# Ten gated branch tiles split inside the head pairs and loaded back as halves; the sum over positions as adds; a new order in the last pair

## The reference

```
h = rms_norm(x) ; z = h @ w_in                       # 2048 -> 6144: u, g_pool, q, k, v, g_attn
pool branch : mean over the last 2/4/8/16 positions - u, a 256x256 map per group, scale, * silu(g_pool)
attn branch : 16 heads x 64, keys at distances 0, d, 2d, .. <= window for (128,1), (512,4), (2048,16),
              penalty -slope*distance, the three patterns weighted by their softmax sums, * silu(g_attn)
x = x + [pool ; attn] @ w_out ; y = rms_norm(x)
```

## Time and profile before

| what | value |
|---|---|
| median of 3 runs | 886.05 us (885.88 to 886.07) |
| the profiled execution's own time | 882.29 us |
| its span, first to last instruction | 880.5 us |
| PE busy | 850.8 us (97%) |
| DVE, ACT, POOL busy | 557.0 us (63%), 396.0 us (45%), 35.0 us (4%) |
| mean granted TensorE clock | 0.988 of full |
| DMA traffic | 117.13 MB, mean 133 GB/s |

### The profile page before, as it was taken

How to read it: one execution, slowest core, us unless ns; L and a number is a source line. 1 busy time by engine, 2 the same in 40 slices (tenths; PEclk the granted TensorE clock), 3 DMA queues, 4 the chain that set the end, 5 groups by cost and what they waited for, 6 DMA issues and landing times. The chain is left out here.

```text
span 880.5 us, 17273 instructions
## 1 busy us (share of the span) xinstructions
PE 850.8 (97%) x6974; PEld 843.1 (96%) x6974; DVE 557.0 (63%) x1067; ACT 396.0 (45%) x917; POOL 35.0 (4%) x62
## 2 busy tenths in 40 slices
PE   7999999999999999999999999999798999999993
PEld 7999999999999999999999999999788999999993
DVE  5646885696678569757956774787788443333333
ACT  5745435524543453355245434533445453433332
POOL 3000000000000000000000000000000000000001
PEclk9999999999999999999999999999899999999997
DMA  9476257337524733663376247326454433433425
GB/s 305 124 144 164 82 144 175 94 93 177 153 73 107 197 107 96 159 151 95 90 177 158 79 126 176 106 77 167 118 167 145 125 111 112 125 113 109 141 65 194
DMA packets 205063, 117.13 MB, mean 133 GB/s; under 512 B 6232, under 2 KB 200288, under 8 KB 204960
## 3 DMA queue, kind: packets, MB, share of 16 engines
q1 hardware_dynamic: 202712, 111.20, 46.8%
q0 software_dynamic: 2272, 4.83, 1.6%
HBM read 103.93 MB, written 12.53 MB: 132 GB/s over the span
## 5 line engine op out<-in xcount | busy, mean ns | idle before, releaser
L578 PE MATMUL pj<-mov_hi,w_hi 128*128 128x260 f32 x1952 | 404.3, 288 | 0.0
L578 PE MATMUL pj<-mov_hi,w_lo 128*128 128x260 f32 x1952 | 393.7, 283 | 0.0
L578 PE MATMUL pj<-mov_lo,w_hi 128*128 128x260 f32 x1952 | 393.1, 283 | 0.0
L578 PEld LDWEIGHTS pj<-mov_hi,w_hi 128*128 128x128 f32 x1952 | 301.5, 189 | 0.9
L578 PEld LDWEIGHTS pj<-mov_lo,w_hi 128*128 128x128 f32 x1952 | 302.0, 189 | 0.0
L578 PEld LDWEIGHTS pj<-mov_hi,w_lo 128*128 128x128 f32 x1952 | 301.7, 189 | 0.0
L1180 DVE TENSOR_TENSOR w_lo<-w_raw,w_hi 128x768 fp32r<-128x768 f32 (+1 forms) x189 | 163.4, 865 | 180.8 <-ACT w_hi L797 179.9
L797 ACT ACTIVATE w_hi<-w_raw 128x768 fp32r<-128x768 f32 (+1 forms) x189 | 145.5, 770 | 200.5 <-PE pj L578 170.0
L853 ACT ACTIVATE pt_hi<-ps_t 128x128 fp32r<-128x128 f32 (+1 forms) x64 | 26.2, 435 | 69.7 <-PE ps_t L607 67.0
L1263 DVE TENSOR_TENSOR pt_lo<-ps_t,pt_hi 128x128 fp32r<-128x128 f32 (+1 forms) x64 | 29.6, 483 | 36.5 <-ACT pt_hi L853 36.5
L845 ACT ACTIVATE arena<-arena,stat 128x128 f32<-128x128 f32 (+1 forms) x64 | 34.2, 558 | 35.2 <-DVE stat L1257 35.1
(11 more groups left out here) (210 smaller groups left out, 801.7 us busy)
## 6 DMA issues: line engine op xcount, KB each, us to landing
w_raw<-in_w_in SPq DMA_DIRECT2D x96, 320.0 KB, 3.5
w_raw<-in_w_in SPq DMA_DIRECT2D x48, 384.0 KB, 3.5
arena<-in_cache_k_win SPq DMA_DIRECT2D x16, 384.0 KB
arena<-in_cache_v_win SPq DMA_DIRECT2D x16, 384.0 KB
w_raw<-in_w_out SPq DMA_DIRECT2D x16, 384.0 KB, 3.3
w_raw<-in_w_out SPq DMA_DIRECT2D x16, 320.0 KB, 3.0
arena<-in_cache_k_win SPq DMA_DIRECT2D x8, 512.0 KB
arena<-in_cache_v_win SPq DMA_DIRECT2D x8, 512.0 KB
```

The lines of the kernel that those rows point to most:

```text
L578: mm = pe.matmul(dst[h][:, 0:HT], w, m[:, k, HT * h:HT * h + HT], start=(k == 0 and i == 0), stop=(c == 2 and k == KT - 1 and i == 2))
```

## The change

1. Ten branch tiles (`STAGED`) are split inside the pairs. ACT copies the tile into `stg_hi` (`stage_hi`), DVE subtracts into `stg_lo` (`stage_lo`), and POOL stores both to DRAM (`send_split`). ACT waits with the next one until both stores of the one before have landed. In the order of pairs: tile 8 (stored in pair 1), 9, 10, 3, 11, 12, 4, 5, 13, 14. Tiles 4, 5 and 13 all come in pair 6, at places 3, 5 and 8; tile 14 comes in pair 7 at place 8.
2. SP loads these halves back straight into `mov_hi` and `mov_lo` (`load_split`): places 3, 4, 5 at step 143, 6, 7, 8 at 144, 9, 10 at 145, 13, 14 at 146. Each group waits until the chunk that last reads these places is done.
3. Three tiles (0, 1, 2) still come through `mix_scratch` and are split at steps 142 (two) and 143 (one).
4. `value_sum` becomes six adds in two parts, at places 22 and 23 (before: 22).
5. In all pairs the key loads are issued at places 5, 6 and 7, and the two small exponentials of the sample rows on ACT go from ahead of the weight split to behind it.
6. In pair 7 the plan is new.

```
-SPLIT_ORDER = (0, 1, 2, 3, 4, 5, 6, 7, 8, 9, 10, 13, 14, 11, 12, 15)
-RELOADED = (0, 1, 2, 3, 4, 5, 6, 7, 8, 9, 10, 13, 14)
-MIX_BUFS = 6
+SPLIT_ORDER = (0, 1, 2, 11, 12, 15)
+RELOADED = (0, 1, 2)
+STAGED = (8, 9, 10, 3, 11, 12, 4, 5, 13, 14)
...
-             vm=(20, 21, 21), vr=22, av=24, pick=25, mix=(19, 21), gate=20)
-FINAL = Plan(qk=(7, 11), s=(8, 12), kn=13, ur=14, kq=(9, 10, 11), ns=15, pt=17,
-             vm=(12, 13, 14), vr=15, av=18, pick=20, mix=(17, 18), gate=19)
+             vm=(20, 21, 21), vr=(22, 23), av=24, pick=25, mix=(19, 21), gate=20)
+FINAL = Plan(qk=(7, 11), s=(8, 12), kn=13, ur=14, kq=(8, 9, 10), ns=17, pt=19,
+             vm=(13, 14, 14), vr=(18, 20), av=20, pick=21, mix=(17, 18), gate=19)
...
+            def load_split(i):
+                k = OUT_K[i]
+                c = 0 if i < 6 else (1 if i < 11 else 2)
+                sp.wait_ge(stg_st, 32 * len(STAGED))
+                sp.wait_ge(w_used, IN_CHUNKS - 1 + c)
+                sp.dma_start(mov_hi[:, i, :].bitcast(F32), hi_dram[k]).then_inc(mov_in[i], 16)
+                sp.dma_start(mov_lo[:, i, :].bitcast(F32), lo_dram[k]).then_inc(mov_in[i], 16)
...
-                    if j in (6, 7, 8):
-                        load_keys(pr, j - 6)
+                    if j in (5, 6, 7):
+                        load_keys(pr, j - 5)
...
+                for i in {-1: (3, 4, 5), 0: (6, 7, 8), 1: (9, 10), 2: (13, 14)}.get(n, ()):
+                    load_split(i)
...
-                        pe.wait_ge(m_split, after_split(k))
+                        if k in mov_in:
+                            pe.wait_ge(mov_in[k], 32)
+                        else:
+                            pe.wait_ge(m_split, after_split(k))
...
+            def stage_hi(k, src):
+
+                e = STAGED.index(k)
+                if e > 0:
+                    act.wait_ge(stg_st, 32 * e)
+                act.activation(stg_hi[:, :], src, ACT.Copy).then_inc(stg_hi_done, 1)
...
+            def send_split(k):
+                pool.wait_ge(stg_split, STAGED.index(k) + 1)
+                pool.dma_start(hi_dram[k], stg_hi[:, :].bitcast(F32)).then_inc(stg_st, 16)
+                pool.dma_start(lo_dram[k], stg_lo[:, :].bitcast(F32)).then_inc(stg_st, 16)
...
+            def add_positions(pr, i, to, n, other):
+
+                out = av if to is None else vv[:, P * to:P * (to + n)]
+                to = to or 0
+                if i > 0:
+                    dve.wait_ge(av_add, 5 * pr + i)
+                o = dve.tensor_tensor(out, vv[:, P * to:P * (to + n)], vv[:, P * other:P * (other + n)],
+                                      ALU.add)
+                o.then_inc(av_add if i < 5 else av_done, 1)
+
+            def value_sum(pr, half):
+
+                if half == 0:
+                    dve.wait_ge(pv_s, 3 * pr + 3)
+                    add_positions(pr, 0, 0, 10, 10)
+                    return
+                add_positions(pr, 1, 0, 5, 5)
+                add_positions(pr, 2, 0, 2, 2)
+                add_positions(pr, 3, 0, 1, 1)
+                add_positions(pr, 4, 0, 1, 4)
                 if pr > 0:
                     dve.wait_ge(av_sum, pr)
-                dve.tensor_reduce(av, vv.rearrange("p (s x) -> p x s", x=P), AX_X,
-                                  ALU.add).then_inc(av_done, 1)
+                add_positions(pr, 5, None, 1, POS - 1)
...
+            def stage_lo(k, src):
+                dve.wait_ge(stg_hi_done, STAGED.index(k) + 1)
+                dve.tensor_tensor(stg_lo[:, :], src, stg_hi[:, :].bitcast(F32),
+                                  ALU.subtract).then_inc(stg_split, 1)
```

131 lines of the change are left out of this document (58 added, 73 removed).

## The result

The changed kernel takes **871.86 us** (median of four runs, 871.21 to 872.39), against 885.96 us for the kernel before on the same chip (four runs, 884.14 to 886.07). The ratio is 0.9845, with a 95% interval of 0.9828 to 0.9862: 14.1 us less, where 9.0 were forecast, and 0.6 us outside the range. A rerun on another chip gave 871.94 against 883.89 us, ratio 0.9866 (0.9851 to 0.9882), which is 12.0 us. The changed kernel repeats; the kernel before does not. Most of this part of the document is about that difference.

The account below looks back on a forecast made before the run. PE bounds the kernel, busy 97% of the span, and loses time only to waits and slow clock in pair 7. 2.7 + 2.0 + 1.4 + 2.9 = 9.0 us off the median of 886.05 gave 877.05 us, range 872.5 to 882.0.

Parts of the forecast that it names:

- Staged tiles: Copies and subtracts of ten tiles move into pairs 1 to 7; counted 0, bounds 0 and 1.2 us lost.
- Loads into the operand in time: Twenty transfers of 260 KB replace ten and arrive before chunks 144 and on want them; counted 0.
- Adds: Six adds replace the sum over positions on DVE: about 3.5 us instead of 4.9, counted 0 for PE.
- Gap 2: PE's wait of 1.99 us in pair 7 up to 659.84, behind a late DVE reciprocal; goes, 2.0 us.
- the cap of 13.4 us: All that pair 7 loses in waits and slow clock; nothing the change touches can be worth more.
- gap 3: PE's wait of 2.89 us in pair 7 up to 668.50, for `pooled_lo` from DVE; goes, 2.9 us.
- gap 1: PE's wait of 5.31 us in pair 7 up to 635.91; 2.7 us shorter, between 2.0 and 3.3.
- The clock: Slow stretches behind pair 7's first two waits lose 1.8 and 1.4 us; counted 0 and 1.4 us saved.
- All of pair 7's losses go: Rival: early key load, no slow stretch, DVE stays ahead; 13.4 us less, or 872.6; 13%.
- The key load no faster: Rival: PE stalls one unit earlier in pair 7, its first wait isn't shortened; about 4 us, or 882; 14%.
- the loads into the operand late: Rival: chunk 147 waits for places 6 to 10 and it ends slower; 896 at 120 GB/s; 5%.
- the mere shuffle: Rival: DVE's list is only shuffled, and what leaves three spots delays three others as much; 886; 6%.

Follow-up runs that it names:

- The keys alone: The kernel before with key loads (all pairs) and the last pair's key products a place earlier, nothing else: 879.84 us, ratio 0.9957.
- The fillers: Useless matmuls put in PE's waits of pair 7: kernel before, all three waits 883.64 us, third alone 882.57 us; changed kernel, two waits 871.5 us.

## Why the prediction was wrong

**What held.** PE bounds the kernel and pays only in pair 7: between two executions the whole difference lies between 507 and 664 us. Staged tiles: 0 forecast, about 1 us by T, at the pooling map's gap. Loads into the operand in time: no PE wait for one, 389 GB/s in the window at 656. Adds: 3.5 us forecast, 3.6 measured, worth nothing to PE. Gap 2: 2.0 forecast, 1.99 gone. The places were forecast in part: one wait at L849, but of 1.76 us and not of 2 to 3.3; the first output chunk "some 9 us earlier" (11.0); no wait for `pooled_lo`, where 0.56 or 1.40 us are left.

**What failed, in the order of size.**
- *"I take the gain from the median, since the waits are gaps in the order of work and not noise."* This is the step that put the result outside the range. The prediction took the 3.76 us by which the first median of before stands above its profile as a constant that the changed kernel has too. It hasn't: its median is 0.07 us above its profile. So the 14.1 us are 10.5 from profile to profile and 3.6 of this excess, and the cap of 13.4 us, counted in one execution, didn't hold for medians. What the excess is made of stays open in the main. Over 80 runs the median of before is 883.7, so 2.3 us of the 14.1 lie in the four runs of the first comparison (885.96), which left no trace of what they had. In the rerun the difference is 12.0. Of the 1.4 us that remain over the profile the traces show possible sources (half rate behind gap 3, 3.05 us in an execution that has it; a key load whose landing varies by up to 1 us ahead of gap 1; a start 1.6 us later), but no run shows how much of it the change takes away. "A measurement of this kernel tells 0.2%" doesn't hold for single runs or for three of them: the runs of before span 0.65% (880.96 to 886.71). From profile to profile the sum was short by 1.5 us: gap 1 gave 0.85 more, the clock 0.7 and the unexplained work 0.9, gap 3 gave 0.6 less, and 0.4 was lost outside T.
- *Gap 1, 2.7 us, "the middle" of 2.0 and 3.3.* It lost 3.55. The load was issued 6.4 us earlier than the third one before (4.3 were forecast) and was there when DVE came, and DVE never waited. It gave a little more than the better end. The keys alone gave 3.13.
- *The clock, 1.8 and 1.4 us.* Windows of 4 us cut the stretches at their edges; in windows of half a microsecond they are 2.1 and 1.7. After the change 1.7 is left in the profiled execution, and none in the rerun's: 2.1 saved for 1.4 forecast. And these microseconds were counted as if each were time. The fillers show that a stretch ahead of another wait is mostly free.
- *Gap 3, 2.9 us.* 0.56 is left in one trace, 1.40 in another. The prediction had `pooled_lo` 0.9 us ahead of PE. It came at 656.82, 1.0 us earlier even than 660.5 less the 2.7 of gap 1, but PE was ready at 657.05, 2.4 us earlier than 662.2 less the same 2.7. Counted from the end of gap 1, `pooled_lo` moved by 6.7 us and not by 7.2.

**The rivals.** "All of pair 7's losses go" has nearly the right number (13.4 us, 872.6) and the wrong mechanism: a gap of 1.76 us and a half-rate stretch stay, and what makes the number is where the first median of the kernel before lay. That its number comes out is luck. The key load no faster, the loads into the operand late, and the mere shuffle didn't occur. The sign that the prediction named for a gain over 9 us, full clock behind gap 1, was absent in one trace and present in another, with T 0.7 us apart and the same time to 0.1 us.
